# GpSimd's multiplication by the softmax ratio as a tensor-scalar operation, and another split of columns between VectorE and GpSimd

## The reference, cut to what matters

```
bias = tbl[t5_bucket(kpos[None, :] - qpos[:, None])]
s = jnp.einsum('bqhcd,bkhcd->bhcqk', qblk, kf) + bias[None, :, None]
pr = jax.nn.softmax(s, axis=-1)
w = pr[:, :, 0] - lam * pr[:, :, 1]
return jnp.einsum('bhqk,bkhe->bqhe', w, vf)
```

## Time and profile before

| | us |
|---|---|
| median of 3 runs | 1035.57 |
| the profiled execution's own time | 1035.5 |
| its span, first to last instruction | 1033.7 |
| TensorE busy | 1003.1 (97%) |
| VectorE busy | 655.1 (63%) |
| ScalarE busy | 580.7 (56%) |
| GpSimd busy | 496.4 (48%) |
| DMA, mean over the span | 145 GB/s |

### The profile page before, as it was taken

The page is one execution under the profiler, slowest core; times in us unless marked ns, Lnnn a source line. Parts: engine busy times, 40 slices in busy tenths (PEclk is TensorE's granted clock), DMA queues, the critical chain, the costliest instruction groups (busy, mean ns, idle before and its releaser), DMA issues.

```text
span 1033.7 us, 15465 instructions
## 1 busy us (share of the span) xinstructions
PE 1003.1 (97%) x5792; PEld 796.5 (77%) x5792; DVE 655.1 (63%) x1055; ACT 580.7 (56%) x890; POOL 496.4 (48%) x404
## 2 busy tenths in 40 slices
PE   7999999999999999979999999999899999999997
PEld 6877777777788888857777777777788888888886
DVE  4654948493583350379999999999965344445423
ACT  7738485845641231379999999999842221112112
POOL 1233243626567440056677677666676344353421
PEclk9999999999999999999999999999999999999999
DMA  9651543323265538659687487343384222432321
GB/s 339 245 171 36 173 147 103 117 82 133 62 184 168 158 86 217 204 139 248 164 203 205 107 208 192 93 130 124 114 279 148 87 87 99 148 100 87 107 81 41
DMA packets 105929, 150.34 MB, mean 145 GB/s; under 512 B 10232, under 2 KB 68728, under 8 KB 105848
## 3 DMA queue, kind: packets, MB, share of 16 engines
q1 hardware_dynamic: 105712, 149.36, 48.0%
q10 hardware_dynamic: 144, 0.00, 0.0%
HBM read 102.07 MB, written 44.11 MB: 141 GB/s over the span
## 4 chain that ended last, share of the span: by engine, by line
PE 75%; DVE 16%; issue 7%; ACT 1%; DMA 1%; SPq 0%; DVEq 0%; POOLq 0%; POOL 0%; ACTq 0%
DVE E_ L1643 11%; PE b_ps L1819 6%; PE b_ps L1922 6%; PE b_ps L1924 6%; PE b_ps L1923 6%; PE b_ps L1821 6%; PE b_ps L1820 6%; PE g_ps L1819 4%; PE g_ps L1821 4%; PE g_ps L1820 4%; PE o_ps L1985 3%; PE w_ps L1968 2%; PE h_ps L1819 2%; PE uT_ps L1873 2%; PE h_ps L1821 2%
## 5 line engine op out<-in xcount | busy, mean ns | idle before, releaser
L1254 ACT ACTIVATE E_<-E_,nmax 128x1024 f32<-128x1024 f32 (+1 forms) x184 | 186.7, 1018 | 14.9 <-DVE nmax L1643 14.7
L1643 DVE CUSTOM_DVE_ANT_0 E_<-s_ps,bias 128x1024 f32<-128x1024 f32 (+1 forms) x184 | 188.0, 1057 | 3.6 <-PE s_ps L1935 3.6
L972 POOL TENSOR_TENSOR E_<-E_,ratio 128x576 f32<-128x576 f32 (+3 forms) x92 | 84.5, 918 | 85.8 <-DVE E_ L1659 85.8
L1821 PE MATMUL b_ps<-u_hi,wA_lo 128*128 128x512 f32 x288 | 112.3, 390 | 0.0
L975 POOL TENSOR_TENSOR E_<-E_ 128x576 f32<-128x576 f32 (+3 forms) x92 | 103.7, 1127 | 7.2
L1935 PE MATMUL s_ps<-KL,QL 128*128 128x512 f32 x256 | 90.7, 435 | 13.8 <-DVE nmax L1643 13.0
L1819 PE MATMUL b_ps<-u_hi,wA_hi 128*128 128x512 f32 x240 | 95.4, 398 | 4.0 <-DVE u_lo L1413 3.4
L1820 PE MATMUL b_ps<-u_lo,wA_hi 128*128 128x512 f32 x240 | 93.5, 390 | 0.0
L1968 PE MATMUL w_ps<-ident,E_ 128*128 128x128 f32 x624 | 83.5, 273 | 1.7 <-ACT WT L1285 1.7
L1285 ACT ACTIVATE WT<-w_ps 128x1024 f32<-128x1024 f32 (+1 forms) x96 | 83.4, 868 | 2.8 <-PE w_ps L1968 2.6
L1968 PEld LDWEIGHTS w_ps<-ident,E_ 128*128 128x128 f32 x624 | 72.6, 140 | 14.8 <-issue 3.8
(11 more groups left out here) (228 smaller groups left out, 2316.4 us busy)
## 6 DMA issues: line engine op xcount, KB each, us to landing
QL<-qk_t SPq DMA_DIRECT2D x32, 256.0 KB, 6.8
KL<-qk_t SPq DMA_DIRECT2D x32, 256.0 KB, 8.2
bias<-line_d SPq DMA_DIRECT2D x8, 960.0 KB, 11.7
x_sb<-in_x SPq DMA_DIRECT2D x12, 512.0 KB, 9.0
z_ch<-z_stage SPq DMA_DIRECT2D x24, 256.0 KB, 2.5
qk_t<-qh SPq DMA_DIRECT2D x24, 256.0 KB, 2.3
qk_t<-ql SPq DMA_DIRECT2D x24, 256.0 KB, 2.8
mf<-mix_t SPq DMA_DIRECT2D x24, 256.0 KB, 4.0
```

What stands on the lines that cost most here:

```text
L1254: act.activation(e, e, ACT.Exp, bias=nmax[:, n % 5, c:c + 1], scale=-1.0, accum_out=sums[:, n % 5, c:c + 1]).then_inc(e_done, 1)
L1643: dve.tensor_tensor_reduce(weights_at(n)[:, c, 0:n_tok], s_ps[:, c, 0:n_tok], b[:, ::-1], -1.0, 3e38, ALU.add, ALU.min, nmax[:, n % 5, c:c ...
L1821: mm = pe.matmul(dst, sl, mh, start=False, stop=k == n - 1)
```

## The change

It has two parts. GpSimd's multiplication of its columns of E1 by ratio, until now an operation of two tensors (with ratio broadcast to the shape of the tile), becomes an operation of one tensor and a scalar per partition. And the split moves: in class (1, 1) GpSimd gets 704 columns in place of 576, in (1, 0) 320 in place of 256, in (0, 0) 320 in place of 256. Class (0, 1), with 384, and the last three steps, with 192, stay. VectorE's columns are the rest of 1024 or 512. The semaphores and the order of instructions stay the same.

```diff
@@ split_at(n) @@
-            return {(1, 1): 448, (1, 0): 768, (0, 0): 256, (0, 1): 128}[(int(long_now), int(long_next))]
+            return {(1, 1): 320, (1, 0): 704, (0, 0): 192, (0, 1): 128}[(int(long_now), int(long_next))]
@@ combine(n) on GpSimd @@
                 gp.wait_ge(w_dve, n + 1)
-                gp.tensor_tensor(two, two, ratio[:, n % 4:n % 4 + 1].to_broadcast([P, n_tok - split_at(n)]),
-                                 ALU.mult).then_inc(scaled, 1)
+                gp.tensor_scalar(two, two, ratio[:, n % 4:n % 4 + 1], None, ALU.mult).then_inc(scaled, 1)
                 gp.wait_ge(scaled, n + 1)
                 gp.tensor_tensor(one, one, two, ALU.add).then_inc(w_gp, 1)
```

## The result

The changed kernel takes 1095.47 us (median of 4 runs, 1095.13 to 1095.8), against 1035.66 us for the kernel before on the same chip (4 runs). The ratio is 1.0575, with a 95% interval of 1.0562 to 1.0589. It is 59.8 us slower, where 5.5 us faster was forecast.

A forecast was written before the change was run, and what follows sets the result against it. The prediction took a loop through GpSimd, whose addition holds VectorE's ratio, to bound the attention's long steps. Gains of 2.0 + 3.0 + 0.5 = 5.5 us, from 1035.5 us profiled, gave a forecast of 1030.0 us, range 1026 to 1036.

The forecast's parts named there:

- What bounds the kernel now: Attention's long steps: a loop through GpSimd, whose addition holds VectorE's ratio (0.35 us against 0.22), sets the 3.47 us period.
- (a): VectorE's combine: 1.04 ns a column, so 128 fewer columns save 0.133 us in each of 47 long steps.
- (b): GpSimd's addition: from 576 to 704 columns at 2.17 ns a column, 1.43 to 1.707 us; 0.873 at 320.
- (c): GpSimd's multiplication as a tensor_scalar: 907 ns for 704 columns, against 1147 for 576 in the kernel before.
- The new loop: Long steps through GpSimd: 3.38 us a step instead of 3.47, still above VectorE's own 3.21, saving 0.09 us.
- (d): 15 of 47 long intervals where VectorE also normalises: VectorE sets them, the full 0.133 us is saved, 2.0 us.
- (e): Steps around the change to the short sequence: first 768-column combine saves 0.5 us over 7 heads; the rest is hidden.
- (f): Class (0, 1) and the last three steps: split kept, multiplications 0.04 to 0.2 us shorter each, nothing waits for them.
- Rival C: Attention's long steps: multiplication at the broadcast form's rate, 1361 ns, GpSimd's loop 3.83 us, 11.5 us slower, 1047; chance 0.14.
- A: Attention's long steps: multiplication at most 0.74 us, VectorE's 3.21 sets the period, 10.8 us gained, 1024.7; chance 0.12.
- B: Attention heads: TensorE takes the slack, a third kept, 1.8 us gained, 1033.7; chance 0.12, including Rival C's middle prices.

The follow-up runs named there:

- split_544: The kernel before with GpSimd's share in class (1, 1) cut from 576 to 544 columns, nothing else: 1033.85 us, ratio 0.998.
- ratio_before: The kernel before with VectorE's ratio as a tensor_scalar of one tensor and two scalars per partition: 1034.26 us, ratio 0.9983.
- ratio_one_input_look: The changed kernel with VectorE's ratio as a tensor_scalar of one tensor and two scalars, run again for an undisturbed profile: 1073.22 us, single execution.
- forms: A kernel without the layer, timing GpSimd's operations alone at 1 to 1024 columns: at 704, scalar multiplication took 2042 ns with one operation, 857 with two.
- two_op: The changed kernel with GpSimd's multiplication as a tensor_scalar of two operations (by 1.0, then by ratio): 1029.1 us, ratio 0.9937.
- split_only: The kernel before with the new split, GpSimd's multiplication kept in the broadcast form: 1048.95 us, ratio 1.0122.

## Why the prediction was wrong

- **What bounds the kernel now: right.** The loop of ratio, combine, multiplication and addition was read from 0.13 us of extra duration in a one-column instruction. split_544 (fewer columns for GpSimd, faster), ratio_before (the extra time is gone with the second SBUF input) and ratio_one_input_look (the hold moves to the next instruction with two) show it, and these runs are against a semaphore as the cause, since no wait was touched. The Trainium skill (SBUF — State Buffer, Who interferes with whom) has a VectorE instruction contend with a GpSimd one that reads SBUF when it has two SBUF inputs, and not with one. By that rule, the trace agrees: 1.54 us held with two, 0.27 with one.
- **(a) and (b), VectorE's columns and the addition: right**, within 10 ns.
- **(c), the multiplication: the step that failed.** "Then 704 columns are 265 + 31 + 703 x 0.87 = 907 ns"; it measured 2045. The slope was taken from the rows of 1 and 16 columns. Those instructions multiply and add, and the new one only multiplies. The rows of eight columns (234 for one operation, 203 for two) did show that the two are not the same, and I took the difference as a fixed 31 ns. In forms it is 34 ns at one column and then grows with every column: 2.50 ns against 0.84. The upper end, the broadcast form's rate with surcharges (1450), did not bound it either; nothing in the rows excluded a scalar form slower than the broadcast one. The loop of 3.38 us and the 3.0 us gained in 32 steps rest on this term.
- **The new loop.** With 2.045 in the place of 0.907, the prediction's own sum is 0.637 + 2.045 + 0.07 + 1.707 + 0.06 = 4.52 us. It measured 4.53. Without the wrong term, in two_op, it gave 3.38 with 907 and 3.33 with 857, and 3.35 was measured; the time came out at 1029.1 where 1030.0 was forecast.
- **(d), VectorE's 15 longer intervals: right for the forecast, not for the result.** In two_op they shrink by 0.14 and 0.13 us, as forecast. At 4.53 us all 47 intervals belong to the loop, the ones with a normalisation too (547.61 to 552.12, 4.51).
- **(e), the short steps.** "0.1 more in a step of over 2 us, also hidden" went with the price of (c): 320 columns take 1085 + 869 ns. The rests of the heads cost 14 us. In the four heads with wa_low GpSimd's own queue adds to it: while the subtraction at 583.54 runs (1.28 us), the combine of 192 columns at 583.63 takes 1.40 us, where the one at 581.03 takes 0.42.

```profile
583.54 1.28 POOL L979 TENSOR_TENSOR wa_lo<-wa_raw,wa_hi 128x512 fp32r<-128x512 f32 x1
583.63 1.40 DVE L1658 SCALAR_TENSOR_TENSOR E_<-E_,ratio 128x192 f32<-128x192 f32 x1
```

- **(f), the classes whose split stayed.** That "their multiplications get 0.04 to 0.2 us shorter each" rests on the same price, and the sign was wrong: 384 columns take 1244 ns instead of 825, and 192 take 915 instead of 632.
- **Rival C** had the mechanism and the direction, at a chance of 0.14, and 1047 as its time. That number is right for its own premise: split_only, the broadcast form's rate with the new split, took 1048.95. But the premise stopped at the broadcast form's rate, and the true rate lay beyond it. Rivals A and B are out. B's fear is not seen in two_op either, where the gain of 6.8 us passed through nearly whole (7.0 expected).
- **The sentences of the skill.** One-input operations at roughly line rate (GPSIMD Engine Reference, When to use GPSIMD) would be an estimate of 0.83 ns a column: the trace agrees for the form with two operations (0.84), and disagrees for the one with one (2.50). The estimate of 1.5 from 1.8 cycles an element (Performance versus the Vector engine) was met by neither; the measured rates decide.

The range, too, went wrong with (c): its high end of 1036 had room only for multiplications up to about 1.1 us, though the widest measured one stood at 16 columns.

## What to carry to other kernels

A price for a new form of an instruction must come from the same form: the same number of operations and the same kinds of operand, at a width near the one needed. Where no such row exists, its cost is open upwards, above the form that it replaces too, and the width of the range should say so. When two engines take turns at one port, add up what each holds it for in a step; in the kernel before, a column moved from VectorE (1.04 ns) to GpSimd (1.67 + 2.17 ns) makes that sum larger, and helps only while GpSimd ends before VectorE needs the port.

## What the runs showed of the hardware

- GpSimd's tensor_scalar with one operation costs 2.50 ns a column (float32, 128 partitions, 2042 ns at 704), and with two operations 0.84 (857 ns), both with a scalar per partition. At 704 columns, multiplying by 1.0 first makes the multiplication 2.4 times as fast.
- A one-column VectorE instruction with two SBUF inputs takes 0.22 us alone and up to 1.55 us when it meets a GpSimd addition; its duration grows, and no wait is shown. With one tensor and two scalars per partition it took 0.27 to 0.28 us in all 96 steps of each kernel that has it, also beside an addition.
- Of a held VectorE combine, only the time of its columns comes after GpSimd's instruction: it ended 0.35 us after it with 320 columns, 0.74 with 704 and 0.21 with 192, and 1.04 ns a column gives 0.33, 0.73 and 0.20.
- A scalar per partition in place of an immediate adds 69 to 76 ns to GpSimd's tensor_scalar at every width from 1 to 1024 columns (857 against 784, 2042 against 1967).
